# Two weight units of each later stage get their high parts by converting loads from GpSimd instead of copies on ScalarE

## What is computed

```
for i in range(2):
    f = swiglu(rmsnorm(h, ffn1_pre_g[i]), ffn1_w_in[i], ffn1_w_down[i])
    h = h + 0.5 * rmsnorm(f, ffn1_post_g[i])
    hn = rmsnorm(h, mix_pre_g[i])
    mixed = gmlp_and_ssd(hn) if i % 2 == 0 else mla_attention(hn)
    h = h + rmsnorm(mixed, mix_post_g[i])
    f = swiglu(rmsnorm(h, ffn2_pre_g[i]), ffn2_w_in[i], ffn2_w_down[i])
    h = h + 0.5 * rmsnorm(f, ffn2_post_g[i])
    gate = sigmoid(rmsnorm(h, ple_pre_g[i]) @ ple_w_gate[i])
    h = h + rmsnorm(gate * (p[i] @ ple_w_proj[i]), ple_post_g[i])
```

## Time and profile before

| what | value |
|---|---|
| median of three runs | 1113.64 us |
| the profiled execution's own time | 1113.49 us |
| its span, first to last instruction | 1111.8 us |
| PE busy | 1100.2 us |
| VectorE (DVE) busy | 817.8 us |
| ScalarE (ACT) busy | 569.5 us |
| GpSimd (POOL) busy | 82.6 us |
| read from HBM over the span | 206.39 MB |
| DMA engines, queue of SP | 48.9% |
| DMA engines, queue of GpSimd | 3.6% |

### The profile page before, as it was taken

The page is one execution under the profiler, slowest core; times in us unless marked ns, Lnnn a source line. Parts: engine busy times, 40 slices in busy tenths (PEclk is TensorE's granted clock), DMA queues, the critical chain, the costliest instruction groups (busy, mean ns, idle before and its releaser), DMA issues.

```text
span 1111.8 us, 14127 instructions
## 1 busy us (share of the span) xinstructions
PE 1100.2 (99%) x5724; PEld 937.1 (84%) x5724; DVE 817.8 (74%) x1074; ACT 569.5 (51%) x706; POOL 82.6 (7%) x138
## 2 busy tenths in 40 slices
PE   8999999999999999999999999999999999999997
PEld 6888888887888888888888888888888888888886
DVE  5786777588997677677786867768876667776775
ACT  7444444567564554444565544445775555444453
POOL 3200000200110200000113000001200020000011
PEclk9999999999999999999999999999999999999999
DMA  8755555645544555555555555554523365555551
GB/s 316 256 190 189 189 190 187 253 169 188 187 174 152 209 218 189 190 189 190 189 199 221 193 190 189 190 190 176 203 76 115 123 246 185 192 188 192 191 170 57
DMA packets 31600, 208.37 MB, mean 187 GB/s; under 512 B 3760, under 2 KB 3808, under 8 KB 8112
## 3 DMA queue, kind: packets, MB, share of 16 engines
q1 hardware_dynamic: 27936, 194.00, 48.9%
q0 software_dynamic: 3600, 13.46, 3.6%
HBM read 206.39 MB, written 1.06 MB: 187 GB/s over the span
## 4 chain that ended last, share of the span: by engine, by line
PE 95%; DVE 1%; issue 1%; DMA 1%; ACT 1%; POOL 0%; SPq 0%; DVEq 0%; POOLq 0%
PE PS L708 24%; PE PS L186 17%; PE PS L188 17%; PE PS L187 17%; PE PS L711 12%; PE PS L383 1%; PE PS L1930 1%; PE PS L1226 1%; PE PS L1951 1%; PE PS L1932 1%; DMA h<-x 1%; DVE WL L168 0%; PE PS L1941 0%; DMA raw<-stream 0%; ACT WH L161 0%
## 5 line engine op out<-in xcount | busy, mean ns | idle before, releaser
L168 DVE TENSOR_TENSOR WL<-raw,WH 128x2048 fp32r<-128x2048 f32 x180 | 411.3, 2289 | 150.4 <-ACT WH L161 149.8
L161 ACT ACTIVATE WH<-raw 128x2048 fp32r<-128x2048 f32 x180 | 342.8, 1907 | 115.2 <-DMA raw<-stream 115.2
L708 PE MATMUL PS<-X,WH 128*128 128x512 f32 x1152 | 288.3, 392 | 0.0
L708 PEld LDWEIGHTS PS<-X,WH 128*128 128x128 f32 x1152 | 209.1, 189 | 38.8
L711 PEld LDWEIGHTS PS<-X,WL 128*128 128x128 f32 x1152 | 157.2, 190 | 11.3
L711 PE MATMUL PS<-X,WL 128*128 128x256 f32 x1152 | 160.6, 282 | 0.0
L812 ACT ACTIVATE sgb<-sgb 128x256 f32<-128x256 f32 x72 | 30.1, 418 | 228.0 <-DVE sgb L808 228.0
L186 PE MATMUL PS<-WH,X 128*128 128x512 f32 (+3 forms) x360 | 141.0, 392 | 0.4 <-DVE WL L168 0.4
L188 PE MATMUL PS<-WL,X 128*128 128x512 f32 (+3 forms) x360 | 138.6, 385 | 0.0
L187 PE MATMUL PS<-WH,X 128*128 128x512 f32 (+3 forms) x360 | 138.5, 385 | 0.0
L186 PE MATMUL PS<-WH,BH 128*128 128x512 f32 x288 | 113.1, 393 | 0.0
(11 more groups left out here) (280 smaller groups left out, 1314.8 us busy)
## 6 DMA issues: line engine op xcount, KB each, us to landing
raw<-stream SPq DMA_DIRECT2D x181, 1024.0 KB, 4.8
PG<-post_g POOLq DMA_DIRECT2D x8, 512.0 KB, 6.7
QG<-pre_g POOLq DMA_DIRECT2D x7, 512.0 KB, 7.5
raw<-stream SPq DMA_DIRECT2D x4, 512.0 KB, 6.9
Eg<-acs_rows POOLq DMA_DIRECT2D x2, 1024.0 KB, 6.8
h<-x SPq DMA_DIRECT2D x4, 256.0 KB, 6.2
out<-h SPq DMA_DIRECT2D x4, 256.0 KB, 2.0
wsT<-gm_w POOLq DMA_DIRECT2D x1, 512.0 KB, 8.9
```

Of the source, the lines that this page charges most:

```text
L161: act.activation(WH[:, n % RING, :], raw[:, n % RING, :], ACT.Copy).then_inc(sem("w_hi"), 1)
L168: dve.tensor_tensor(WL[:, n % RING, :], raw[:, n % RING, :], WH[:, n % RING, :], ALU.subtract).then_inc(sem("w_lo"), 1)
L708: pe.matmul(PS[:, bank, :], wh[:, kt, cols], X[:, kt, :, :].rearrange("p a n -> p (a n)"), start=kt == 0, stop=False)
```

## The change

Units m+2 and m+3 of each stage from s = 1 on, 14 of 183, are no longer copied by ScalarE. GpSimd issues a second load of the same unit from HBM, from float32 into the fp32r tile WH, so that the conversion is to take place during the transfer. SP still loads the unit into raw. Both loads of a unit wait for the same count of w_used. The load of m+2 stands in GpSimd's queue ahead of the old stage's first inverse root, that of m+3 between the first and the second. VectorE, which waited for ScalarE's count, waits for the two landings of these units instead. ScalarE's split_to passes over them.

Some loads now share a semaphore, to make room for the two new ones: dt_w counts with hy_small, and gm_g, gm_b, q_g and kv_g with gains_in. None of these loads moves.

```diff
+        loaded_high = {first[r] + 2 + i: (f"high{i}", 16 * r) for r in range(1, NS) for i in range(2)}
+
+        def load_high(pool, n):
+
+            pool.wait_ge(sem("w_used"), n - RING + 1)
+            pool.dma_start(WH[:, n % RING, :], a["stream"][n, :, :]).then_inc(sem(loaded_high[n][0]), 16)
+
+        def copied_high(n):
+
+            return n - 2 - sum(m <= n for m in loaded_high)
+
         def split_hi(act, n):
-            if n >= n_units:
+            if n >= n_units or n in loaded_high:
                 return
             act.wait_ge(sem(f"raw{n % RING}"), 16 * (n // RING + (1 if n % RING > 1 else 0)))
             act.activation(WH[:, n % RING, :], raw[:, n % RING, :], ACT.Copy).then_inc(sem("w_hi"), 1)
...
-            dve.wait_ge(sem("w_hi"), n - 2)
+            if n in loaded_high:
+                dve.wait_ge(sem(f"raw{n % RING}"), 16 * (n // RING + (1 if n % RING > 1 else 0)))
+                dve.wait_ge(sem(loaded_high[n][0]), loaded_high[n][1])
+            else:
+                dve.wait_ge(sem("w_hi"), copied_high(n))
...
         def boundary_pool(pool, s):
             if s:
+                if s < NS:
+                    load_high(pool, first[s] + 2)
                 post_inverse_rms(pool, s - 1, 0)
+                if s < NS:
+                    load_high(pool, first[s] + 3)
                 post_inverse_rms(pool, s - 1, 1)
...
             split_to(u + 3)
-            act.wait_ge(sem("hy_dtw"), 16)
+            act.wait_ge(sem("hy_small"), 48)
             act.activation(dt_hi, dt_w[:, :, :], ACT.Copy).then_inc(sem("hy_dth"), 1)
-            act.wait_ge(sem("hy_small"), 32)
...
-            pool.dma_start(gm_g[:, :], a["gm_g"].partition_broadcast(P)).then_inc(sem("hy_gm"), 16)
-            pool.dma_start(gm_b[:, :], a["gm_b"].partition_broadcast(P)).then_inc(sem("hy_gm"), 16)
+            pool.dma_start(gm_g[:, :], a["gm_g"].partition_broadcast(P)).then_inc(sem("gains_in"), 16)
+            pool.dma_start(gm_b[:, :], a["gm_b"].partition_broadcast(P)).then_inc(sem("gains_in"), 16)
```

More of the change, by code:

```diff
@@ L133, in sem @@
             return sems[name]
-        for name in ("raw0", "raw1", "raw2", "raw3", "raw4", "w_hi", "w_lo", "w_used", "x_in00", "x_in01", "x_in10", "x_in11", "zeros", "consts", "pg", "qg", "qg_cols", "w_part0", "w_part1", "w_part2", "w_part3", "x_piece", "w_part_hi", "w_lo_half",
+        for name in ("raw0", "raw1", "raw2", "raw3", "raw4", "w_hi", "high0", "high1", "w_lo", "w_used", "x_in00", "x_in01", "x_in10", "x_in11", "zeros", "consts", "pg", "qg", "qg_cols", "w_part0", "w_part1", "w_part2", "w_part3", "x_piece", "w_part_hi", "w_lo_half",
                      "out_done", "ple_done", "post_sq", "post_ms", "post_y", "post_rs", "h_new", "pre_sq", "pre_rs", "hn_done",
@@ L899, in ffn_dve @@
                     dve.wait_ge(sem("hy_wsm"), 2)
-                    dve.wait_ge(sem("hy_small"), 32)
+                    dve.wait_ge(sem("hy_small"), 48)
                     dve.tensor_reduce(RSUM, wsL[:, :, :], mybir.AxisListType.X, ALU.add).then_inc(sem("hy_rsum"), 1)
@@ L1122, in hybrid_trunk @@
         RSUM = EA[:, 0:8]
-        for name in ("hy_small", "hy_rsum", "hy_off", "hy_dtw", "hy_gm", "hy_ws", "hy_wsm", "hy_ng", "hy_ev", "hy_trx", "hy_cx", "hy_pad",
+        for name in ("hy_small", "hy_rsum", "hy_off", "gains_in", "hy_ws", "hy_wsm", "hy_ng", "hy_ev", "hy_trx", "hy_cx", "hy_pad",
                      "hy_ca", "hy_conv", "hy_dth", "hy_dtl", "hy_dtp", "hy_both", "hy_dtc", "hy_dtt", "hy_dtv", "hy_na", "hy_ex",
@@ L1392, in offsets @@
                 act.wait_ge(sem("hy_rsum"), 1)
-                act.wait_ge(sem("hy_gm"), 32)
+                act.wait_ge(sem("gains_in"), 32)
                 act.wait_ge(sem("hy_conv"), 3)
@@ L1550, in gate_v @@
                 if c == 0:
-                    dve.wait_ge(sem("hy_gm"), 32)
+                    dve.wait_ge(sem("gains_in"), 32)
                 chain(dve.tensor_tensor(vt[:, c, :], flat_pair((P1, P2)[c]), gm_g[:, :], ALU.mult))
@@ L1687, in hyb_early @@
         def hyb_early(pool):
-            pool.dma_start(dt_w[:, :, :], a["dt_w"]).then_inc(sem("hy_dtw"), 16)
+            pool.dma_start(dt_w[:, :, :], a["dt_w"]).then_inc(sem("hy_small"), 16)
             pool.dma_start(sm[:, 0:68], a["hy_cols"]).then_inc(sem("hy_small"), 16)
@@ L1773, in hybrid_trunk @@
         MAXS = msm[:, 136:200]
-        for name in ("ml_in", "ml_cm", "ml_cg", "ml_sq", "ml_rs", "ml_cn", "ml_tr", "ml_chi", "ml_clo", "ml_krT",
+        for name in ("ml_in", "ml_cm", "ml_sq", "ml_rs", "ml_cn", "ml_tr", "ml_chi", "ml_clo", "ml_krT",
                      "ml_S", "ml_mx", "ml_nm", "ml_exp", "ml_P", "ml_PT", "ml_PTe", "ml_O", "ml_Ohi", "ml_Olo",
@@ L2215, in mla_dve @@
             x_low(dve, s, 1, (1,))
-            dve.wait_ge(sem("ml_cg"), 32)
+            dve.wait_ge(sem("gains_in"), 64)
             latents(0)
@@ L2259, in mla_early @@
                                base=0, pattern=[[-1, P]], channel_multiplier=1).then_inc(sem("ml_cm"), 1)
-            pool.dma_start(cg[:, 0:Q_LORA], a["q_g"].partition_broadcast(P)).then_inc(sem("ml_cg"), 16)
-            pool.dma_start(cg[:, Q_LORA:Q_LORA + KV_LORA], a["kv_g"].partition_broadcast(P)).then_inc(sem("ml_cg"), 16)
+            pool.dma_start(cg[:, 0:Q_LORA], a["q_g"].partition_broadcast(P)).then_inc(sem("gains_in"), 16)
+            pool.dma_start(cg[:, Q_LORA:Q_LORA + KV_LORA], a["kv_g"].partition_broadcast(P)).then_inc(sem("gains_in"), 16)
         def mla_pool(pool, s):
```

## The result

The changed kernel takes 1116.7 us (median of 10 runs, 1116.01 to 1117.96) against 1113.64 us for the kernel before (10 runs, 1113.27 to 1115.82). The ratio is 1.0023, with a 95% interval of 1.0015 to 1.0032: slower by some 2.6 us. (The ratio is one of means; the two medians are 3.1 us apart.) The span of the profiled execution is 1115.0 us instead of 1111.8.

A forecast was written before the change was run, and what follows sets the result against it. The prediction took TensorE (PE), busy 99% of the span, as the bound. Its only nonzero term, +1.5 us at s=4, on 1113.49 us gave 1115.0, or 1115.1 us at the median; range 1113.2 to 1122.0 us.

The forecast's parts named there:

- the forecast's own case: Loss at s=4 of +0.3 to +3.2 us, chance 0.60: 0.46 within 2.2 us, 0.14 above.
- Step (a): ScalarE loses two copies at each of seven boundaries: gain 0 at the six ordinary ones, at most 0.44 us at s=4.
- Step (b), the term of the sum: At s=4 unit 100's converting load lands at 587.1, so VectorE and PE run 1.5 us later: +1.5 us.
- its upper bound: At s=4 unit 100's converting load lands after 9.9 us, at 588.8, making the term +3.2 us.
- Step (b), plain price for a converting load: GpSimd's converting 1 MB loads take as long as plain ones, 6.2 to 7.5 us; cost 0 at ordinary boundaries.
- rival 2: At s=4 unit 100's converting load lands early and the stall goes: 1113.2 to 1113.9 us, chance 0.10.
- Step (c), the late root: At s=4 the first root starts 0.8 us late, x_low 0.6 us late; not added, eaten by the later stall.
- Step (d): VectorE's wait on two DMA semaphores costs 0; unit 99's load at s=4 has 0.5 us of cover.
- a sign of being wrong: VectorE waiting for DMA at an ordinary boundary, or a PE hole anywhere but the predicted ones at s=4.
- 1, slower conversion: Converting holds the DMA engines longer: about 1122 us if double, past 1130 if three times; chance 0.25.
- 3, gain by ScalarE's relief: Relief pays off through evacuations or the mixer's chains by over 2.2 us; chance 0.02.
- 4, a load that does not round: WH holds plain numbers and WL zeros; same instructions, bytes and time, 1115 us; chance 0.03.

The follow-up runs named there:

- e1: The changed kernel with s=4 left out, ScalarE's copies of units 99 and 100 kept there: 1113.66 us, ratio 0.9998 to the kernel before.
- e2: The change at s=4 alone, 2 converting loads instead of 14: 1116.79 us, ratio 1.0025 to the kernel before.
- e7: The changed kernel, but SP issues raw load 101 at s=4 only after unit 100's converting load has landed: 1115.44 us, ratio 1.0015 to the kernel before.
- e5: The changed kernel, but at s=4 ScalarE copies unit 99 as before and only unit 100 converts: 1116.06 us, ratio 1.0019 to the kernel before.
- e11: The changed kernel, but at s=4 ScalarE copies unit 99 and raw load 101 waits for unit 100's converting load: 1114.31 us, ratio 1.0006 to before.
- e3: The changed kernel, but at s=4 GpSimd does the first inverse root ahead of load_high(m+2): 1117.16 us, ratio 1.0032 to the kernel before.
- e6: The changed kernel, but GpSimd's two loads at s=4 go plain into unused memory and ScalarE copies these units again: 1117.36 us, ratio 1.0030 to before.
- e9: The changed kernel, but at the six ordinary boundaries each converting load is issued behind its inverse root: 1120.76 us (4 runs), ratio 1.0052 to before.
- e8: The changed kernel with, at s=4, raw load 101 held until unit 100's converting load landed and the first root ahead of load_high(m+2): 1117.46 us, ratio 1.0024.
- e4: The changed kernel, but at s=4 ScalarE copies unit 100 as before and only unit 99 converts: 1115.45 us, ratio 1.0013 to the kernel before.

## Why the prediction was right, and where it was off

**Sign and place: right, and shown.** The forecast was +1.5 us, all of it at the step from ple into s=4, through high 100's landing. e1 and e2 show the place, e7, e5 and e11 the mechanism. The size is less good: the measured change, about 2.6 to 3.1 us, is nearly twice the forecast. It lies in the stated range, but beyond the 2.2 us to which I had given the greater chance, in the upper part of the forecast's own case (+0.3 to +3.2).

**Step (a), no gain at ordinary boundaries: right.** e1 has the whole relief of ScalarE at six boundaries and the time of before.

**Step (b), the term of the sum: mis-sized.** It put VectorE's start of unit 100 at 587.1; it was 588.10, and PE's transposes 2.5 us late instead of 1.5. The 4.99 us from there to the transposes held (5.01), and the landing as counted from the issue was nearly right, 8.4 for 8.2 us. What failed is the start that I counted from: issue at 578.9, measured 579.60. 0.44 us of this is SP's load too (579.33): w_used came late because PE was late. 0.27 us is GpSimd's issue behind SP's. But e3 shows that this is no cause to be removed: with an earlier issue the landing takes longer. So that 8.2 us came out right has some luck in it. What counts is when the DMA engines are through with 5 MB from 574.3 on, and that is 588. The prediction had the better sum at hand: five loads at its 2.6 us each are 13 us, and 13.7 were measured from the first issue. It counted from high 100's issue instead and took 8.2 us between two bounds; its upper bound, all work ahead of high 100 in a row, 588.8, misses by nearly as much to the other side (0.8 us) as 587.1 does (0.9).

**Step (b), plain price for a converting load: right, and shown** by e6 in landing times. The lower end, 6.2 us, did not bound it though: with no load at its side a 1 MB load from GpSimd landed after 5.0 to 5.3 us in e9. The Trainium skill's formula in rival 2 ("DMA: Bandwidth & Descriptors", "Anatomy of one DMA") gives 4.4 us and is nearer to 5.0 than my row was, but at s=4 nothing is alone and the 8.4 us stand.

**Step (c), the late root: right twice.** It was 1.0 us late (0.8 forecast), PE was 1.0 us late at the stage's start (0.6 forecast), and this is eaten by the later stall: e3 against the change, e8 against e7. I had dropped this after seeing the trace, for the 0.44 us of late issue, and the run put it back.

**Step (d): right as to its own wait.** High 99 landed at 581.60, VectorE came at 582.51. But the cost of 0 holds only for that wait: e4 shows that high 99, with the root late behind it and raw 100 landing late beside it, costs 1.35 us where unit 100 is copied.

**What the sum lacked.** Between the transposes and the end another 0.8 us appears in the change, in e3 and in e5, 0.6 in e2 and 0.5 in e4 and e7. Of this 0.34 us was lost at one place in the change, where PE's products at 616.37 wait for actb (L838): they began 1.29 us after the group before them, instead of 0.95. ScalarE's copy of a unit whose load had just landed stands ahead of actb. This is a hole away from the touched units, which the prediction named as a sign of being wrong, though a small one. e1 shows 0.34 us with s=4 untouched, so part of the 0.8 us is scatter between executions; the rest stays open.

**Rivals.** 1, slower conversion, is excluded. 2, an early landing, did not occur, and e11 comes closest: with raw 101 out of the way the landing is early enough to leave only +0.4 us. 3, gain by ScalarE's relief, is excluded by e1 for anything near its 2.2 us. 4, a load that does not round, would give the same time, and no run here tells it apart.

## What to carry to other kernels

Taking work off an engine brings nothing where the engine that ends the span does not wait for it: look at what the next engine's idle time says ahead of each touched instruction, not at the busy share. Moving work from an engine to DMA is free only where the transfer has cover counted in bytes: sum what is in flight beside it from the first issue on and divide by the full rate, above all where a ring is emptied in a burst and the loads come close behind one another. And when one engine's lateness is followed by a longer stall with another cause, it is eaten; adding the two, or repairing the first, moves nothing.

## What the runs showed of the hardware

A load that converts float32 to fp32r took no longer than a plain one of the same size from the same queue: 7.0 us beside one SP load in both cases, 8.4 to 8.9 against 9.2 with more in flight. A GpSimd load of 1 MB landed after 5.0 to 5.3 us alone (e9), and after 7.0 to 7.2 beside an SP load issued 0.2 to 0.3 us ahead of it (the change, eleven of the twelve loads at ordinary boundaries; the last took 8.5). With a second SP load 1.6 us behind it, at s=4, it took 8.3 to 9.2.

The opening varies. PE's granted clock, from the view by stretches of 9 to 13 us, first the kernel before, then e7:

```profile
9.00:13.00 4.00, 4.00 (x23) 3.32 (x22) 3.37 (x9) 3.67 (x11) 0.00 (x0) 1.00 1.06 437
```

```profile
9.00:13.00 4.00, 4.00 (x16) 3.05 (x14) 2.35 (x5) 2.54 (x7) 0.00 (x0) 0.69 1.04 428
```

In e7 a part of this stretch ran at the lower level of 1.2 GHz, 16 matmuls instead of 23 began, and everything after was 1.7 us late. What PE did before it: it had stood still for the first input, for 2.2 us in e7 and 1.6 us in the kernel before.

```profile
PE PS L400 <- DMA h<-x: 2.2, 1, 2.2
```

The thirteen traces fall into two groups by it. In seven (e1, e2, e3, e5, e7, e8, e9) PE waited 2.0 to 2.2 us for the first input, the granted clock from 9 to 13 us was 0.57 to 0.73, and the first boundary's transposes began at 193.4 to 194.0. In the other six the waits make 1.0 to 1.6 us, the clock was 1.00, and the transposes began at 191.4 to 191.9. That the wait is what lowered the clock was not tested by a run of its own.
